# Moving two state updates of a hybrid decoder step from the router's top-4 into the first expert matmuls

## The chip, the cores and the metric

The kernel runs on one core of a Trainium2 chip. The metric is the device time of one execution in microseconds (us). The kernel before took 1251.17 us, the median of three executions (1255.02, 1241.98 and 1251.17 us).

## The reference: what is computed

One inference step of one decoder layer for a prompt group (256 tokens) and a sample group (8 sequences of 4 tokens, 32 tokens), all in float32, with the same weights:

```
x = x + W_out [GatedDeltaNet heads | GLA heads](RMSNorm(x))
x = x + MoE(RMSNorm(x))          # 32 experts, top 4, D = FF = 1024
y = RMSNorm(x)
# GLA, per token:  S_t = diag(e^{gk_t}) S_{t-1} + k_t v_t^T ,  o_t = S_t^T q_t
#   state_gla: (1, 8 sequences, 4 heads, 64, 128), updated and returned as gla_sample
# MoE, per token:  logits = x @ w_router + b_router; top 4; gates = softmax(top 4)
#   gu = x @ w_up[e] + b_up[e]; act = (clip(up)+1) * gate * sigmoid(1.702 gate); act @ w_down[e] + b_down[e]
```

The weights of the 32 experts (w_up 8 MB and w_down 4 MB each) are nearly everything that is read from memory. The new GLA states of the eight sample sequences are an output of their own: nothing later in the layer reads them.

## The kernel before, in words

Each engine has a program written out by hand, and semaphores join them. The first 250 us compute the projections, the convolution and both mixers. Then come the output projection with the router (to about 302 us), and the experts.

**Experts.** They go in 16 pairs (`two_experts`, for both experts of a pair). A pair's weights are twelve units of 2 MB: units 0 to 3 are w_up of the first expert (q = 0), 4 to 7 w_up of the second (q = 1), 8 to 11 w_down. A ring of eight slots holds them (`load_unit`, L362, issued by SyncE). SyncE issues a unit's load when the matmuls that read the slot's last content have signalled (`w_used`, `p_up`, `p_yd`), one after another in one order. In `up` (L1021) a unit, which the change's title calls a piece, is 8 matmuls of 512 columns, recorded as 16; `down` (L1047) is built alike. Between them stand `gather` (L1056: it collects the rows of the tokens that chose the experts, by a matrix `G` of zeros and ones that VectorE writes), transposes (L548) and `scatter` (L972: it adds a pair's result to the tokens).

**The first pair** is written out ahead of the loop. Unit 8 of it doesn't go to the ring: it lies in eight spare places (`extra`, L386), of 256 KB each. Places 6 and 7 are in the buffer `xb`, where the masked keys of the second GLA update (`kgm[1]`) lie until `state_update(5)` has read them; so SyncE waits for `p_up_s` 6 ahead of them.

**State updates.** There are six, 0 to 3 for the delta heads and 4 and 5 for two GLA heads each. `state_update(h)` (L860) does a 32-row outer product per sequence and head into two banks, and signals `p_up_s`. VectorE adds the banks to the decayed state in `states(h)` (L1400: two additions of 128x512) and signals `st_ok`. Updates 4 and 5 use banks 7, 2 and 4, 3. At `st_ok` 6 GpSimd writes `sls` out (L533) and, when that has landed, loads `b_down` in its place (L535), which the last pair needs.

**The router.** VectorE reads the logits (L1487) and makes the top-4 selection in small steps (L1490 to L1502), up to `route_ok`. TensorE waits for this, then counts the positions of the tokens in the experts' lists (L960, L962, signal `p_pos`). VectorE makes `G` of them (L1510 to L1555), TensorE gathers the first half of the rows (L1056, `gather(0, 5)`), ScalarE copies them (L1843), and the first `up` begins. Between its second unit and its third stand `gather(1, 4)`, which writes bank 4 and waits for `st_ok` 6, and `gates_t`. `keep_warm(b, n)` (L556) does n matmuls of the identity with 512 columns into bank b; nobody reads them.

Of the kernel before, what the change touches and what calls it, by code (L numbers as in the profile page):

```python
# [36 lines left out]
def program(nc, a, o):  # L37
    ctx = ExitStack()
    with ctx:
# [3 lines left out]
        def sem(name):  # L43
            return ctx.enter_context(nc.semaphore(name))
# [187 lines left out]
        def used(i, n):  # L232

            name, at = [("w_used", 1), ("w_used", 2), ("w_used", 3), ("p_up", 1), ("w_used", 4), ("w_used", 5), ("w_used", 6), ("p_up", 2),
                        ("w_used", 7), ("p_yd", 1), ("w_used", 8), ("p_yd", 2)][n]
            return name, i * (8 if name == "w_used" else 2) + at

        def place(n, odd, first=False):

            return (n - RING if n > RING else (n + 1) % RING) if first else (n + 4 * odd) % RING  # L240

        def landed(k, n, odd, first=False):

            return (16 if n < RING - 1 else 32) if first else k * 48 + 16 * ((n + 12 * odd) // RING + 1)
# [17 lines left out]
        sems = {n: sem(n) for n in names}  # L262
# [38 lines left out]
        def _(sp):  # L301
# [53 lines left out]
            def load_unit(p, n, odd, first=False):  # L355

                if n < 8:
                    src = up[p * 2 + n // 4, n % 4 // 2, :, UNIT * (n % 2):UNIT * (n % 2 + 1)]
                else:
                    src = dn[p * 2 + (n - 8) // 2, n % 2]  # L360
                s = place(n, odd, first)
                sp.dma_start(slot[WSLOT[s]], src).then_inc(sems[f"ld_w{s}"], 16)  # L362
# [18 lines left out]
            for m in range(8):  # L381
                if m == 2:
                    sp.wait_ge(sems["p_lg"], 3)
                if m == 6:
                    sp.wait_ge(sems["p_up_s"], 6)
                sp.dma_start(extra[m], dn[0, 0, :, 512 * m:512 * (m + 1)]).then_inc(sems["ld_w0" if m == 0 else "ld_extra"], 16)  # L386

            for n in range(9, 12):
                name, value = used(0, n - 9)
                sp.wait_ge(sems[name], value)  # L390
                load_unit(0, n, 0, True)
            for n in range(5):
                name, value = used(0, n + 3)
# [149 lines left out]
        def _(pe):  # L543
# [115 lines left out]
            for t in range(NTT):  # L659
                n = TN[t]  # L660
# [86 lines left out]
            for t in range(NTT):  # L747
                n = TN[t]
# [5 lines left out]
            for k, (l, t) in enumerate(INV):  # L754
                n = TN[t]
# [93 lines left out]
            def state_update(h):  # L849

                pe.wait_ge(sems["kdm_ok"], h + 1)
                for b in range(NB):
                    out_b = bank[ST_BANKS[h][b // 4]]
                    cols = slice((b % 4) * P, (b % 4) * P + P)
                    if h < 4:
                        i = pe.matmul(out_b[:, cols], kdm[h][0:SMP, b, :], vn[0:SMP, 2, h * P:(h + 1) * P], start=True, stop=True)
                    else:
                        for r in range(2):
                            hh = 2 * (h - 4) + r
                            i = pe.matmul(out_b[64 * r:64 * r + 64, cols], kgm[h - 4][b // 4][0:SMP, b % 4, 64 * r:64 * r + 64],  # L860
                                          vg[0:SMP, 2, hh * P:(hh + 1) * P], start=True, stop=True)
                c.tick(i, "p_up_s")
# [28 lines left out]
            def logits(t, j):  # L891

                at = XT.index((t, j))
                if at < 5:
                    pe.wait_ge(sems["xnT_ok"], at + 1)
                else:
                    pe.wait_ge(sems["lgT_ok"], 1)
                for m in range(4 * j, 4 * j + 4):
                    i = pe.matmul(bank[LG_BANKS[t]][0:TN[t], 0:E_N], hT[:, m, TO[t]:TO[t] + TN[t]], wr[:, m, :],
                                  start=m == 0, stop=m == KT - 1, skip_group_check=True)  # L900
                if j == 1:
                    c.tick(i, "p_lg")
# [45 lines left out]
            columns(1, 1)  # L948
            keep_warm(0, 1)
            logits(1, 1)  # L950
            state_update(4)
            state_update(5)

            pe.wait_ge(sems["route_ok"], 1)
            pe.wait_ge(sems["tri_ok"], 3)
# [19 lines left out]
            def gates_t():  # L975

                pe.wait_ge(sems["gat_ok"], 1)
                pe.wait_ge(sems["lg_ok"], 5)
                for t in range(NTT):
                    ins = turn(bank[5][0:E_N, TO[t]:TO[t] + TN[t]], gates[0:TN[t], E_N * t:E_N * (t + 1)], TN[t])  # L980
                ins.then_inc(sems["p_gT"], 1)
# [13 lines left out]
            def up(i, q, k, odd, first=False, last_w=None):  # L995

                pe.wait_ge(sems["sel_ok"], i * 2 + (q + 1))
                for g in range(2):
                    rows_ = slice(64 * g, 64 * g + 64)
                    pe.matmul(bank[2 * q + g][:], sels[q][rows_].rearrange("p h c -> p (h c)"), b_gu[rows_], start=True, stop=False,  # L1000
                              skip_group_check=True)
                for u in range(4):
                    n = 4 * q + u
                    if first and q == 0 and u == 2:
                        pe.wait_ge(sems["st_ok"], 6)
                        gather(1, 4)
                        gates_t()
                    if first and q == 0 and u == 0:
                        pe.wait_ge(sems["lgT_ok"], 2)
                    elif first and q == 0 and u == 1:  # L1010
                        pe.wait_ge(sems["xe_ok"], 1)
                    elif q == 0 and u % 2 == 0:
                        pe.wait_ge(sems["xe_ok"], i * 2 + (u // 2 + 1))
                    s = place(n, odd, first)
                    pe.wait_ge(sems[f"ld_w{s}"], landed(k, n, odd, first))
                    w = slot[WSLOT[s]].rearrange("p (k g h n) -> p k g h n", k=2, g=2, h=2)
                    for kk in range(2):
                        at = 2 * u + kk
                        for g in range(2):
                            for h in range(2):  # L1020
                                last = pe.matmul(bank[2 * q + g][CAP * h:CAP * (h + 1), :], xeT[:, at, q * CAP:(q + 1) * CAP], w[:, kk, g, h, :],  # L1021
                                                 start=False, stop=at == KT - 1, skip_group_check=True)
                    last.then_inc(sems["w_used" if u < 3 else "p_up"], 1)
                    if last_w is not None and u > 0:
                        bias_pair(i, last_w, u - 1)
# [25 lines left out]
            def gather(j, b):  # L1051

                for n in range(4):
                    for t in range(NTT):
                        at = (4 * j + n) * P
                        last = pe.matmul(bank[b][:, n * P:(n + 1) * P], ot[:, t, at:at + P], G[:, t, :], start=t == 0, stop=t == NTT - 1)  # L1056
                last.then_inc(sems["p_gat"], 1)
# [53 lines left out]
        def _(v):  # L1111
# [16 lines left out]
            for t in range(NTT):  # L1128
                n = TN[t]
# [109 lines left out]
            for t in range(NTT):  # L1239
                if t == 1:  # L1240
                    g_diffs(2)
                n = TN[t]
# [11 lines left out]
            for t in range(NTT):  # L1254
                n = TN[t]
                m = upi if t < 2 else upis
                c.done(v.tensor_tensor(Dtt[t], Dtt[t], bc(m.unsqueeze(1), n, H, n), ALU.mult), "d_ok")
            for t in range(NTT):
                n = TN[t]
# [7 lines left out]
            for t in range(NTT):  # L1267
                n = TN[t]
# [14 lines left out]
            for t in range(NTT):  # L1283
                n = TN[t]
# [37 lines left out]
            for k, (l, t) in enumerate(INV):  # L1322
                n = TN[t]
# [71 lines left out]
            def states(h):  # L1395
                v.wait_ge(sems["p_up_s"], h + 1)
                v.wait_ge(sems["dec_ok"], h + 1)
                for k in range(2):
                    st = sgs[:, 4 * k:4 * k + 4, h, :] if h < 4 else sls[:, h - 4, 4 * k:4 * k + 4, :]
                    i = v.tensor_tensor(st, st, bank[ST_BANKS[h][k]][:].rearrange("p (b d) -> p b d", b=4), ALU.add)  # L1400
                c.done(i, "st_ok")
# [82 lines left out]
            for t in range(NTT):  # L1484
                n = TN[t]
# [16 lines left out]
            c.done(v.tensor_tensor(selm[:], gts[:], eqs[:], ALU.add), "route_ok")  # L1502

            c.done(v.memset(posm[:], 0.0), "v_step")
            states(4)
            v.wait_ge(sems["p_pos"], 1)
            for t in range(NTT):
                n = TN[t]
# [3 lines left out]
            def pick_gu(q, e):  # L1512

                v.tensor_copy(sels[q], bc(twos[:, :, bass.ds(e, 1)], P, 2, CAP)).then_inc(sems["sel_ok"], 1)
# [54 lines left out]
            c.done(v.tensor_reduce(cnt[0:1, 0:1], bank[6][0:1, 0:E_N], AX_X, ALU.max), "lg_ok")  # L1569
            for q in range(2):  # L1570
                pick_gu(q, q)
            states(5)
            v.wait_ge(sems["gexp_ok"], 1)
            c.done(v.tensor_tensor(gates[:], gates[:], selm[:], ALU.mult), "v_step")
            c.done(v.tensor_reduce(den[:], e3(gates), AX_X, ALU.add), "v_step")
# [10 lines left out]
            c.done(v.tensor_scalar(cnt[0:1, 1:2], cnt[0:1, 1:2], 1.0, None, ALU.add), "v_step")  # L1586
            c.done(v.tensor_scalar(cgt[0:1, 0:1], cnt[0:1, 1:2], float(PAIRS // 2), -1.0, ALU.mult, ALU.add), "v_step")
            c.done(v.tensor_copy(rnd[:], cgt[0:1, 0:1]), "rnd_ok")

            def two_experts(i, w, first=False, last=False):  # L1590

# [38 lines left out]
            for t in range(NTT):  # L1630
                n = TN[t]
# [276 lines left out]
```

## Time and profile before

| | |
|---|---|
| median of three executions | 1251.17 us |
| profiled execution, its time | 1243.56 us |
| its span (first to last instruction) | 1241.4 us |
| TensorE busy | 97% of the span |
| VectorE, ScalarE, GpSimd busy | 31%, 17%, 6% |
| read from memory | 428.39 MB, written 4.88 MB |

The profile is of one execution. Its page gives the busy time of each engine, the span in 40 slices of 31 us, the chain of work that ended last and the costliest groups of instructions; the trace gives each instruction with its start, its length and what ended the idle time ahead of it. "Landing" is the time from a transfer's issue to its completion. PEclk is TensorE's granted clock as a share of 2.4 GHz.

### The profile page before, as it was taken

To read this page: it belongs to the slowest core of one execution; us is meant where nothing else is said; L and a number is where in the kernel's file an instruction comes from. 1 tells how busy PE (TensorE), PEld (TensorE's weight loads), DVE (VectorE), ACT (ScalarE), POOL (GpSimd) and SP (SyncE) were. 2 spreads that over 40 slices of the span, in tenths; PEclk is the share of its full clock that TensorE was granted. 3 is DMA by queue.
4 is the path that set the end of the run, shared out by engine and by line. 5 is a ranking of instruction groups with operands and counts; after the bars stand their busy time and mean duration, and the time that the engine had idled before them with its cause. 6 is when DMAs were issued, how large, how long until landed. Compare 5 with 4: busy or idle time off the path is not lost.

```text
span 1241.4 us, 15614 instructions
## 1 busy us (share of the span) xinstructions
PE 1207.3 (97%) x6213; PEld 585.8 (47%) x6213; DVE 380.1 (31%) x802; ACT 215.0 (17%) x522; POOL 72.0 (6%) x114
## 2 busy tenths in 40 slices
PE   6999999899999999999999999999999999999997
PEld 5777787766343433434343434334343434243422
DVE  3676774563112130312212121303112121212133
ACT  2143333322120111101020201111010202020102
POOL 5010103251000000000000000000000000000000
PEclk9999999998999999999999999999999999999999
DMA  9423010289999999999999999999999999999993
GB/s 274 129 87 111 31 69 2 73 318 360 404 413 422 428 429 428 429 428 429 428 429 428 428 428 429 429 428 429 428 429 428 428 429 429 428 429 428 428 428 146
DMA packets 50813, 433.75 MB, mean 349 GB/s; under 512 B 7534, under 2 KB 14010, under 8 KB 26332
## 3 DMA queue, kind: packets, MB, share of 16 engines
q1 hardware_dynamic: 49596, 429.46, 83.5%
q0 software_dynamic: 1184, 3.84, 1.0%
q8 instruction: 23, 0.38, 0.1%
q14 instruction: 10, 0.08, 0.0%
HBM read 428.39 MB, written 4.88 MB: 349 GB/s over the span
## 4 chain that ended last, share of the span: by engine, by line
PE 84%; DMA 9%; DVE 4%; ACT 1%; issue 1%; POOL 0%; DVEq 0%; SPq 0%; ACTq 0%; POOLq 0%
PE bank L1021 33%; PE bank L1047 15%; DMA ring<-in_w_up 8%; PE bank L972 7%; PE bank L1056 6%; PE bank L611 4%; PE bank L548 3%; PE bank L703 3%; PE bank L1000 2%; PE bank L872 2%; PE bank L760 1%; PE bank L769 1%; PE bank L767 1%; PE bank L690 1%; PE bank L723 1%
## 5 line engine op out<-in xcount | busy, mean ns | idle before, releaser
L1021 PE MATMUL bank<-ring,xb 128*64 128x512 f32 x2048 | 448.3, 594 | 4.9 <-DMA ring<-in_w_up 4.0
L1021 PEld LDWEIGHTS bank<-ring,xb 128*64 128x64 f32 x2048 | 144.0, 137 | 304.4 <-issue 296.2
L1047 PE MATMUL bank<-ring,qkv 128*64 128x512 f32 x1008 | 223.3, 595 | 0.7 <-ACT qkv L1834 0.7
L1540 DVE TENSOR_TENSOR qkv<-qkv,bank 128x512 f32<-128x512 f32 (+1 forms) x96 | 65.6, 684 | 241.9 <-PE bank L972 241.9
L1047 PEld LDWEIGHTS bank<-ring,qkv 128*64 128x64 f32 x1008 | 69.6, 137 | 130.7 <-issue 126.2
L972 PE MATMUL bank<-xb,wsm 128*128 128x512 f32 (+1 forms) x192 | 92.9, 620 | 1.7 <-DVE xb L1532 0.9
L1056 PE MATMUL bank<-rowsel,ob 128*128 128x128 f32 x768 | 91.9, 276 | 0.0
L1532 DVE COPY xb<-bank 64x512 f32<-64x512 f32 x16 | 11.1, 695 | 260.6 <-PE bank L1047 260.6
L1056 PEld LDWEIGHTS bank<-rowsel,ob 128*128 128x128 f32 x768 | 89.3, 194 | 2.4 <-DVE rowsel L1555 1.6
L1519 DVE TENSOR_SCALAR xb<-bank 128x512 f32<-128x512 f32 x32 | 21.8, 682 | 206.7 <-PE bank L548 188.8
L611 PE MATMUL bank<-hT,ring 128*128 128x288 f32 x320 | 81.0, 413 | 0.0
L1829 ACT ACTIVATE qkv<-xb 128x512 f32<-128x512 f32 x32 | 20.2, 631 | 342.1 <-DVE xb L1519 340.0
L611 PEld LDWEIGHTS bank<-hT,ring 128*128 128x128 f32 x320 | 61.2, 193 | 17.7 <-issue 0.8
L1839 ACT COPY xb<-bank 64x512 f32<-64x512 f32 x48 | 27.8, 579 | 185.7 <-PE bank L1047 185.3
L972 PEld LDWEIGHTS bank<-xb,wsm 128*128 128x128 f32 (+1 forms) x192 | 25.7, 164 | 67.4 <-DVE qkv L1540 41.7
L538 POOL TENSOR_TENSOR rst<-rst,mhalf 128x1 f32<-128x1 f32 x3 | 2.6, 879 | 915.1 <-DVE rst L1622 915.0
L1823 ACT ACTIVATE xb<-bank,wff 128x128 f32<-128x128 f32 x124 | 35.3, 367 | 53.0 <-PE bank L1056 53.0
L1856 ACT COPY wsm<-bank 128x288 f32<-128x288 f32 x16 | 6.4, 398 | 218.4 <-PE bank L548 218.4
L703 PE MATMUL bank<-hT,ring 128*128 128x288 f32 x128 | 41.1, 436 | 0.1
L1000 PE MATMUL bank<-b_gu,hT 64*128 64x512 f32 x128 | 36.1, 641 | 0.0
L548 PE MATMUL bank<-ident,xb 128*128 128x128 f32 x152 | 28.4, 305 | 1.5 <-DVE xb L1130 1.5
L872 PE MATMUL bank<-ring 128*128 128x512 f32 x64 | 28.4, 597 | 0.4 <-DVE ring L1392 0.4
(355 smaller groups left out, 885.3 us busy)
## 6 DMA issues: line engine op xcount, KB each, us to landing
ring<-in_w_up SPq DMA_DIRECT2D x128, 2048.0 KB, 23.0
ring<-in_w_down SPq DMA_DIRECT2D x63, 2048.0 KB, 26.2
ring<-in_w_in SPq DMA_DIRECT2D x7, 2048.0 KB, 8.3
ring<-in_w_out SPq DMA_DIRECT2D x2, 2048.0 KB, 8.3
ring<-in_state_gdn SPq DMA_DIRECT2D x4, 512.0 KB, 10.2
out<-ring POOLq DMA_DIRECT2D x1, 2048.0 KB, 15.1
xb<-in_x_prompt SPq DMA_DIRECT2D x1, 1024.0 KB, 5.2
sls<-in_state_gla SPq DMA_DIRECT2D x4, 256.0 KB, 7.4
```

What stands on the lines that cost most here:

```text
L548: return pe.transpose(out, src, ident[0:n, 0:n])
L611: i = pe.matmul(bank[at % 4][:, 0:T], w[:, k, n * P:(n + 1) * P], hT[:, k, :], start=k == 0, stop=k == KT - 1)
L703: i = pe.matmul(bank[0][:, 0:T], w[:, k, n * P:(n + 1) * P], hT[:, k, :], start=k == 0, stop=k == KT - 1)
L872: i = pe.matmul(bank[b][:], z, w[:, k, :], start=k == 0, stop=k == KT - 1)
L972: pe.matmul(bank[banks[at]][0:TN[t], :], S[:, TO[t]:TO[t] + TN[t]], yr[:, 512 * j:512 * (j + 1)], start=True, stop=True).then_inc(sems["p_ ...
L1000: pe.matmul(bank[2 * q + g][:], sels[q][rows_].rearrange("p h c -> p (h c)"), b_gu[rows_], start=True, stop=False, skip_group_check=True)
L1021: last = pe.matmul(bank[2 * q + g][CAP * h:CAP * (h + 1), :], xeT[:, at, q * CAP:(q + 1) * CAP], w[:, kk, g, h, :], start=False, stop=at = ...
L1047: last = pe.matmul(bank[5 - q][CAP * h:CAP * (h + 1), :], aTs[q][:, kk, CAP * u:CAP * (u + 1)], w[kk][h], start=u == 0 and kk == 0, stop=u ...
L1056: last = pe.matmul(bank[b][:, n * P:(n + 1) * P], ot[:, t, at:at + P], G[:, t, :], start=t == 0, stop=t == NTT - 1)
L1540: v.tensor_tensor(d, d, bank[banks[at]][0:TN[t], :], ALU.add).then_inc(sems["sc_ok"], 1)
L1823: last = act.activation(xeT[:, k, :], bank[b][:, P * n:P * (n + 1)], ACT.Copy, scale=wff[:, k:k + 1])
L1839: act.copy(yr[CAP * q:CAP * (q + 1), 512 * h:512 * (h + 1)], bank[5 - q][CAP * h:CAP * (h + 1), :]).then_inc(sems["yb_ok"], 1)
```

## The change

Three engines are touched. On TensorE `state_update(4)` and `(5)` leave their place ahead of the wait for `route_ok`; four matmuls of `keep_warm` stand there. Both updates now come in the first `up`, between its second and third unit, ahead of the wait for `st_ok` 6 and `gather(1, 4)`. On VectorE `states(4)` and `states(5)` go from among the selection's steps to behind `rnd_ok`, ahead of the first `swiglu`. On SyncE the loads of units 9 and 10 go ahead of `extra` 6 and 7, whose wait for `p_up_s` 6 now ends later.

```diff
@@ SyncE
                 if m == 6:
+                    for n in range(9, 11):
+                        name, value = used(0, n - 9)
+                        sp.wait_ge(sems[name], value)
+                        load_unit(0, n, 0, True)
                     sp.wait_ge(sems["p_up_s"], 6)
                 sp.dma_start(extra[m], ...)
-            for n in range(9, 12):
+            for n in range(11, 12):
                 ...
@@ TensorE
             logits(1, 1)
-            state_update(4)
-            state_update(5)
+            keep_warm(0, 4)
             pe.wait_ge(sems["route_ok"], 1)
 ...
                     if first and q == 0 and u == 2:
+                        state_update(4)
+                        state_update(5)
                         pe.wait_ge(sems["st_ok"], 6)
                         gather(1, 4)
                         gates_t()
@@ VectorE
             c.done(v.memset(posm[:], 0.0), "v_step")
-            states(4)
             v.wait_ge(sems["p_pos"], 1)
 ...
                 pick_gu(q, q)
-            states(5)
             v.wait_ge(sems["gexp_ok"], 1)
 ...
             c.done(v.tensor_copy(rnd[:], cgt[0:1, 0:1]), "rnd_ok")
+            states(4)
+            states(5)
```

TensorE in the first `up`, from the second unit's last matmuls to the third unit. Before (`ring` is a weight slot, `xb` on its left the gathered rows, `rowsel` holds `G`, `ob` the rows of all tokens):

```order
L1021 MATMUL bank1<-ring,xb 64x512 x2
L1056 MATMUL bank4<-rowsel,ob 128x128 [waits st_ok]
L1056 MATMUL bank4<-rowsel,ob 128x128 x11
L548 MATMUL bank5<-ident,ml 32x128 [waits lg_ok,gat_ok]
L1021 MATMUL bank0<-ring,xb 64x512 [waits ld_w3,xe_ok]
```

With the change:

```order
L1026 MATMUL bank1<-ring,xb 64x512 x2
L864 MATMUL bank7<-xb,qkv 64x128 [waits kdm_ok]
L864 MATMUL bank7<-xb,qkv 64x128 x7
L864 MATMUL bank2<-xb,qkv 64x128 x8
L864 MATMUL bank4<-xb 64x128 [waits kdm_ok]
L864 MATMUL bank4<-xb 64x128 x7
L864 MATMUL bank3<-xb 64x128 x8
L1061 MATMUL bank4<-rowsel,ob 128x128 [waits st_ok]
```

The 32 outer products now stand in the middle of a weight stage, and right behind them TensorE waits for VectorE's last addition.

SyncE's loads at the same place. Before:

```order
L386 DMA hT<-in_w_down 128x512 x3
L386 DMA xb<-in_w_down 128x512 [waits p_up_s]
L386 DMA xb<-in_w_down 128x512
L362 DMA ring<-in_w_down 128x4096 [waits w_used] x3
```

With the change:

```order
L390 DMA hT<-in_w_down 128x512 x3
L362 DMA ring<-in_w_down 128x4096 [waits w_used] x2
L390 DMA xb<-in_w_down 128x512 [waits p_up_s]
L390 DMA xb<-in_w_down 128x512
L362 DMA ring<-in_w_down 128x4096 [waits w_used]
```

Two full loads went ahead of the two small ones; the third stays behind.

## Rows read from the trace of the kernel before

**Rows 1.** The page, part 2: TensorE busy and GB/s, in 40 slices of 31 us.
```profile
PE   6999999899999999999999999999999999999997
GB/s 274 129 87 111 31 69 2 73 318 360 404 413 422 428 429 428 429 428 429 428 429 428 428 428 429 429 428 429 428 429 428 428 429 429 428 429 428 428 428 146
```

**Rows 2.** Busy time by stretch: PE, PEld, DVE, ACT, POOL, clock, DMA share, GB/s.
```profile
340.00:362.00 22.00, 22.00 (x129) 11.42 (x127) 3.40 (x8) 5.64 (x14) 0.00 (x0) 1.00 1.01 426
362.00:366.00 4.00, 4.00 (x20) 1.15 (x16) 0.00 (x0) 0.00 (x0) 0.00 (x0) 1.00 0.88 315
```

**Rows 3.** The chain of waits, late in the expert loop: start us, us, what.
```profile
892.59 5.66 PE bank L972 x12
...
949.43 5.66 PE bank L972 x12
...
970.21 33.79 DMA ring<-in_w_up
...
1125.15 5.66 PE bank L972 x12
```

**Rows 4.** The ring load issued at 356.1 us, and its landing.
```profile
L362 SPq DMA_DIRECT2D ring<-in_w_up x1: 356/356/356, 356.1 to 356.1; - x1
...
DMA to landing us min/median/max: 9.0/9.0/9.0
```

**Rows 5.** The next ring load, issued at 362.8 us, and its landing.
```profile
L362 SPq DMA_DIRECT2D ring<-in_w_up x1: 348/348/348, 362.8 to 362.8; - x1
...
DMA to landing us min/median/max: 8.1/8.1/8.1
```

**Rows 6.** The one after it, issued at 366.3 us, and its landing.
```profile
L362 SPq DMA_DIRECT2D ring<-in_w_up x1: 332/332/332, 366.3 to 366.3; - x1
...
DMA to landing us min/median/max: 9.5/9.5/9.5
```

**Rows 7.** TensorE in order of time: start us, us, line, count [idle before it].
```profile
295.97 1.02 PE L556 MATMUL bank<-qkv,ident 128*128 128x512 f32 x2
...
297.93 1.96 PE L860 MATMUL bank<-xb,qkv 32*64 32x128 f32 x32
299.73 1.91 PE L860 MATMUL bank<-xb 32*64 32x128 f32 x32
302.25 0.64 PE L960 MATMUL bank<-ml,tri 128*128 128x32 f32 x2 [0.61 <-DVE ml L1502]
...
304.86 2.08 PE L556 MATMUL bank<-qkv,ident 128*128 128x512 f32 x2
306.96 3.61 PE L1056 MATMUL bank<-rowsel,ob 128*128 128x128 f32 x24
...
311.56 7.09 PE L1021 MATMUL bank<-ring,xb 128*64 128x512 f32 x32
318.58 2.94 PE L1056 MATMUL bank<-rowsel,ob 128*128 128x128 f32 x24
...
322.76 7.09 PE L1021 MATMUL bank<-ring,xb 128*64 128x512 f32 x32 [0.88 <-ACT xb L1823]
```

**Rows 8.** TensorE's granted clock around it: columns as in Rows 2.
```profile
298.15:301.56 3.41, 3.41 (x64) 3.24 (x60) 3.00 (x13) 3.41 (x4) 1.55 (x4) 1.00 0.99 418
301.56:304.97 3.41, 2.80 (x21) 2.40 (x19) 1.99 (x6) 2.51 (x4) 0.00 (x0) 0.50 1.03 437
304.97:308.40 3.43, 3.40 (x9) 1.83 (x9) 3.15 (x14) 0.00 (x0) 0.00 (x0) 0.50 1.01 430
```

**Rows 9.** VectorE in order of time: columns as in Rows 7.
```profile
302.45 1.28 DVE L1400 TENSOR_TENSOR sls<-sls,bank 128x512 f32<-128x512 f32 x2
305.04 0.63 DVE L1510 SCALAR_TENSOR_TENSOR ml<-bank,ml 128x32 f32<-128x32 f32 x3 [1.30 <-PE bank L962]
...
306.22 0.68 DVE L1555 TENSOR_TENSOR rowsel<-slots_io,pp 128x128 f32<-128x128 f32 x3
```

**Rows 10.** SyncE's loads of `extra` 6 and 7, and their landing.
```profile
L386 SPq DMA_DIRECT2D xb<-in_w_down x2: 327/2172/4017, 301.7 to 302.0; - x2
...
DMA to landing us min/median/max: 16.7/17.0/17.3
```

## The prediction

> **What bounds the kernel now.** I read the page first. TensorE is busy at nine tenths or more in nearly every slice, and memory delivers 428 GB/s in nearly every slice from the thirteenth on [rows 1]. Both look full, so the page can't tell which of them sets the end. The chain of waits can. In the loop, as far as about 949 us, a pair takes 949.43 - 892.59 = 56.84 us, and the chain stays on TensorE. The next three pairs take 1125.15 - 949.43 = 175.72 us together, which is 5.20 us more than 3 x 56.84, and there the chain runs through a weight load [rows 3]. At 428 GB/s a unit of 2 MB takes 2.097/0.428 = 4.90 us, and twelve of them 58.8 us, 1.9 more than TensorE's pair. So TensorE is the faster of the two in the loop: it starts behind the loads, catches up, and from the twelfth pair on is fed unit by unit. Behind 1125 us it sets the end again.
>
> What sets the loads' pace, then? They are saturated unless a slot comes free too late. I looked for a hole in them. The load issued at 356.1 us landed at 365.1, the one issued at 362.8 at 370.9, the one issued at 366.3 at 375.8 [rows 4 to 6]. The last two are 4.9 us apart, as the rate wants; the first two are 5.8. In 362 to 366 us the queues moved 315 GB/s where 426 went ahead [rows 2]. So the load at 362.8 came some 0.9 us too late, since TensorE had not freed the slot. Thus the chain of this execution is: TensorE to 362.8 us, the weight loads to about 1121 us, TensorE to the end. Two things follow. **What TensorE loses ahead of 362.8 us shifts all later landings and the end by the same amount**; the 5.20 us that it waits late don't take it up. What it gains there is worth 0.9 us at most, since then the loads have no hole left. The change lies all ahead of 362.8 us, so I need its sum for TensorE there: call it S.
>
> **The place that is left.** The two updates are 1.80 + 1.91 = 3.7 us of TensorE, from 297.93 to 301.64 us, and behind them it idles 0.61 us for VectorE's selection [rows 7]. The route's end, 302.2 us, doesn't depend on them. Taking them away gives nothing by itself. The four spare matmuls take at most 4 x 1.02 = 4.1 us [rows 7], and end by 302.0, within the selection: cost 0 under that cover, 4.1 us without it.
>
> VectorE's two additions between `route_ok` and `p_pos` (1.28 us from 302.45) ended ahead of its 1.30 us wait for TensorE [rows 9]; taking them away gives 0. The second pair of additions came behind `G`, on no path that `up` waits for: 0.
>
> What can be gained is the clock. It was at 1.2 GHz from 301.56 to 308.40 us, right behind the updates [rows 8]. In it the position matmuls ran from 302.25 to 304.86, 2.6 us, and the first gather took 3.61 us where the second one, at 2.4 GHz, took 2.94 [rows 7]. The spare matmul between them took 2.08 instead of 1.02, but it lies beside VectorE's 1.9 us from `p_pos` to `G` (305.04 to 306.90, [rows 9]). If the clock stays up, the position matmuls save between 0 and half of 2.6, I take 0.7, and the gather 0.7. If it falls at the position matmuls anyway (they are small, and an idle stretch stands ahead of them), nothing is saved. Bounds 0 and 2.0 us (1.3 + 0.7), I take **-1.0 us**.
>
> The Trainium skill's page "TensorE: Matmul & The Clock Gate" (Terms) prices throttled time at the time x (1 - K/N), here 6.8 us x 1/2 = 3.4 us; by it S would be 2.4 us smaller than mine. The rows above show that part of the dip covered idle time and VectorE's steps.
>
> **The place that is new.** Between the second and third unit TensorE does the same 32 products, 3.7 us, and nothing is beside them: **+3.7 us**. Then it waits for `st_ok` 6. Before, that was long there when `gather(1, 4)` came. Now the additions of update 4 (1.28 us) hide behind the products of update 5, and those of update 5 don't: a pair of additions took 1.28 us [rows 9], and a step across engines cost about 0.1 us (`route_ok` and `p_pos` both), twice: **+1.45 us**, bounds 1.3 and 1.6. Behind it stand `gather(1, 4)`, `gates_t`, and every later unit; ScalarE's copy, for which the third unit waited 0.88 us [rows 7], comes as late as the gather does, so that wait stays.
>
> The clock again: the updates ran with TensorE busy in 3.41 of 3.41 us, and the clock fell at the end of that stretch [rows 8]. Now 3.7 us of them and 1.4 us of idling follow each other, so I expect one fall there. If it comes, the gather costs 0.7 more, and if it lasts into the third unit that goes at half pace. Bounds: no fall, 0; a fall as long as before, at half pace for all of 6.8 us, 3.4. I take **+1.25 us**, the gather's 0.7 and half a microsecond of the third unit. The skill's page "TensorE: Matmul & The Clock Gate" (What's actually happening) says that activity releases the throttle, a busy engine staying at full clock; by that rule alone this term is 0 and S is 1.25 us smaller. The first stretch of rows 8 speaks against it: all busy, and down.
>
> **Queues passed.** SyncE now holds `extra` 6 and 7 until `p_up_s` 6, about 321 us instead of 301.7, behind units 9 and 10. They landed 17 us after issue [rows 10], so at about 338 us; the first `down`, the only reader, stands behind six more units, 21 us from the third unit's start (322.76 before, [rows 7]), so at 344 us or later before and later still now. Cost 0. Units 9 and 10 wait for the same signals as before. Unit 11 and all behind it wait for TensorE, whose lateness is S already. The four writes of `sls` and the load of `b_down` go some 13 us later, into the loads of 323 to 327 us; ahead of 362.8 us that only fills room, and the reader of `b_down` is the last pair: 0. VectorE's additions come before its first `swiglu`, for which TensorE needs two more units: 0.
>
> **Sum.** S = -1.0 + 3.7 + 1.45 + 1.25 = **+5.4 us**, from 3.0 (-2.0 + 3.7 + 1.3) to 8.7 (3.7 + 1.6 + 3.4). Against the profiled execution that is 1243.56 + 5.4 = 1249.0 us; against the median of the three others 1256.6. The four executions shown spread over 13 us, far more than S, and their mean is 1247.9; a new median may fall anywhere among them, so I set the forecast at 1247.9 + 5.4 = **1253 us**.
>
> **Rivals.**
> - *The lateness is hidden (0.16).* If the loads have no hole at 362.8 us, for instance since memory is a little slower in a run of 1251 us than in this one, TensorE's lateness is first taken up by the depth of the queue, and its 5.20 us of late waits take the rest. For it: the hole is only 0.9 us, and the chain's longest part is the loads [rows 2, 3]. Against it: with S = 5.4 the slots come so late that a hole opens even there; only 1 to 2 us would be hidden. In full it gives S = 0, about 1248 us.
> - *The early gain wins (0.04).* The clock stays up at both places, TensorE arrives earlier by 2 us, and the updates cost less in the middle of wide matmuls than alone. It would need the 3.7 us to shrink below 0.5; S is then -0.9 at best, 1247 us. The rows speak for 3.7.
> - *The clock stays down (0.05), the other side.* Place: from the third unit on. If, behind 5 us of narrow products and waiting, the clock doesn't return with the gather but stays at 1.2 GHz through the third to sixth unit, these 14.2 us (2 x 7.09, [rows 7]) double: S = 4.15 + 0.7 + 14.2 = 19, 1267 us. It decides from some 8 us of such work on, where S passes 12.5. For it: the dip of rows 8 outlasted the updates by 6.8 us. Against it: it ended as soon as a gather ran.
> - *The late `extra` (0.03).* A load late in the run takes 33.8 us to land [rows 3]; if these two did so here, they would come at 355 us, up to 5 us after `down` wants them (344 + 5.4 at the earliest): up to 1258 us.
>
> The forecast's own case has 0.72.
>
> **Range and chances.** 1243 to 1262 us: the lowest execution shown with most of the least S hidden, up to the highest, 1255, with S at 7. A change under 1% (12.5 us) can't be told from none for this kernel. The forecast and the two rivals with a small S lie within it; beyond it on the slow side is the clock rival with 0.05, and as much for the spread of the medians on top of 5.4 us; beyond it on the fast side only that spread, 0.02.
>
> **What would show it.** In the new profile: spare matmuls at 298 to 301.5 us and no idle time changed ahead of L963; PEclk at 1.00 in 302 to 308 if the first gain is real, and the first `up` starting at about 310.5 instead of 311.56. The updates at about 317.6 to 321.3, then a wait of about 1.4 us on VectorE's `sls`, and a stretch at clock 0.5 between 319 and 326. The third unit at about 328 instead of 322.76. The ring load that was issued at 362.8 at about 368, with its landing 8 us behind it; and the scatter that began at 1125.15 at about 1130.5. I am wrong if the third unit is late but that scatter isn't (hidden), or if the clock is still down at 330 us.

## The result, and the profile after

| | before | with the change |
|---|---|---|
| median of 20 executions each | 1248.08 us | 1252.95 us |
| lowest and highest | 1241.98, 1257.62 | 1249.20, 1263.80 |
| profiled execution, its time | 1243.56 us | 1251.58 us |
| its span | 1241.4 us | 1249.5 us |

The ratio of the changed kernel to the kernel before is 1.0058, with a 95% interval from 1.0036 to 1.0079: 7.2 us slower, from 4.5 to 9.9. The medians lie 4.9 us apart. The forecast was 1253 us: slower, by less than 1%.

The two traces show where it goes. TensorE with the change, in order of time, answers to [rows 7]:

```profile
299.57 3.68 PE L560 MATMUL bank<-qkv,ident 128*128 128x512 f32 x8
303.99 0.41 PE L963 MATMUL bank<-ml,tri 128*128 128x32 f32 x2 [0.73 <-DVE ml L1507]
...
305.60 1.12 PE L560 MATMUL bank<-qkv,ident 128*128 128x512 f32 x2
307.70 5.49 PE L1061 MATMUL bank<-rowsel,ob 128*128 128x128 f32 x24 [0.98 <-DVE rowsel L1559]
313.12 1.32 PE L1003 MATMUL bank<-b_gu,hT 64*128 64x512 f32 x4
314.37 7.09 PE L1026 MATMUL bank<-ring,xb 128*64 128x512 f32 x32
321.39 1.96 PE L864 MATMUL bank<-xb,qkv 32*64 32x128 f32 x32
323.18 1.91 PE L864 MATMUL bank<-xb 32*64 32x128 f32 x32
326.54 4.57 PE L1061 MATMUL bank<-rowsel,ob 128*128 128x128 f32 x24 [1.45 <-DVE sls L1405]
330.95 0.51 PE L552 MATMUL bank<-ident,ml 128*32 128x128 f32 x3
332.34 7.09 PE L1026 MATMUL bank<-ring,xb 128*64 128x512 f32 x32 [0.88 <-ACT xb L1828]
```

The third unit of the first `up` starts at 332.34 us, 9.58 later than before. Piece by piece:
- 1.74 us were lost ahead of the change (303.99 against 302.25). They are no part of it: the section on the hardware comes back to them.
- From the first position matmul to the first unit of `up` it took 10.38 us (314.37 - 303.99), before 9.31 (311.56 - 302.25): +1.07. The position matmuls went faster (1.6 us instead of 2.6), then TensorE idled 0.98 us, and the gather took 5.49 us instead of 3.61.
- From the end of the second unit to the second gather stand 5.15 us that weren't there (321.39 to 326.54): 3.7 of products and 1.45 of waiting for `sls`.
- That gather took 4.57 us instead of 2.94, and to the third unit it was 5.80 instead of 4.18: +1.62.

I call the stretch from the first position matmul to the third unit **the route**. It was 302.25 to 322.76 = 20.51 us, and is 28.35: **+7.84 us by the change**.

The granted clock with the change (columns as in [rows 2]):

```profile
303.99:306.90 2.91, 2.73 (x20) 1.70 (x20) 1.12 (x7) 1.73 (x3) 0.00 (x0) 0.97 1.00 422
306.90:313.70 6.80, 6.00 (x26) 5.68 (x28) 4.00 (x25) 0.47 (x2) 0.00 (x0) 0.51 0.97 380
313.80:327.30 13.50, 12.05 (x106) 6.44 (x103) 2.57 (x4) 0.57 (x3) 0.52 (x1) 1.00 0.75 286
327.50:330.80 3.30, 3.30 (x18) 3.30 (x18) 0.00 (x0) 0.00 (x0) 2.02 (x3) 0.53 0.94 367
```

The first fall didn't go away: it began at about 306.7 us, 2.7 us behind the first position matmul, where in [rows 8] it began 0.7 us ahead of it. It is as long as there, 6.8 us, but now the whole first gather lies in it. A second fall of 3.4 us, from 327.2 us, hit the second gather.

The loads, against [rows 5] and [rows 3]. The ring load that was issued at 362.8 us, and the late end of the chain of waits:

```profile
L362 SPq DMA_DIRECT2D ring<-in_w_up x1: 348/348/348, 372.4 to 372.4; - x1
...
DMA to landing us min/median/max: 7.4/7.4/7.4
```

```profile
959.01 5.66 PE bank L975 x12
979.79 33.82 DMA ring<-in_w_up
...
1134.76 5.66 PE bank L975 x12
```

The load is 9.6 us late, and the scatter that began at 1125.15 us is 9.61 us late. TensorE's late waits took up nothing. The span is longer by only 8.1: late in the kernel before the clock fell for a short while and the last scatter but one took 7.25 us, and here there was no such fall and it took 5.72.

### The profile page after: what moved, and what is told of

It is laid out like the page before. It is cut to its first block, busy times and chain, and to the rows that moved or that the text cites. A ratio compares the mean times of both kernels' runs of the same rounds, so it can differ in the third digit from the quotient of the medians.

```text
span 1249.5 us, 15629 instructions
## 1 busy us (share of the span) xinstructions
PE 1213.6 (97%) x6221; PEld 590.5 (47%) x6221; DVE 380.0 (30%) x802; ACT 214.9 (17%) x522; POOL 72.2 (6%) x114
## 4 chain that ended last, share of the span: by engine, by line
PE 84%; DMA 9%; DVE 5%; ACT 1%; issue 1%; POOL 0%; DVEq 0%; SPq 0%; ACTq 0%; POOLq 0%
PE bank L1026 33%; PE bank L1052 15%; DMA ring<-in_w_up 8%; PE bank L975 7%; PE bank L1061 6%; PE bank L615 4%; PE bank L552 3%; PE bank L707 3%; PE bank L1003 2%; PE bank L876 2%; PE bank L764 1%; PE bank L773 1%; PE bank L771 1%; PE bank L694 1%; PE bank L727 1%
## 5 line engine op out<-in xcount | busy, mean ns | idle before, releaser
L1061 PE MATMUL bank<-rowsel,ob 128*128 128x128 f32 x768 | 95.4, 283 | 2.4 <-DVE sls L1405 1.4
L1061 PEld LDWEIGHTS bank<-rowsel,ob 128*128 128x128 f32 x768 | 92.7, 200 | 3.5 <-DVE rowsel L1559 1.8
```

## The experiments

Each but e4 and e8 is judged by the route in its own profiled execution, since the executions of one kernel spread over 7 to 19 us, and the route leaves out what happened ahead of it. The route repeats well: e8 leaves that part of the kernel before as it was and has 20.50 us, e4 has 20.85, where the kernel before has 20.51. Each kernel has one trace. The excerpts are TensorE in order of time unless said otherwise.

How far a longer route arrives is read from the scatter that began at 1125.15 us before, 822.90 us behind the route's start. In nine of the ten traces with other work on the route (the changed kernel and all runs but e4 and e8) its shift agrees with the route's within 0.5 us; e7 is the tenth.

**e1: the updates left out** (the output `gla_sample` isn't computed).

```diff
# the changed kernel
-                    sp.wait_ge(sems["p_up_s"], 6)
+                    sp.wait_ge(sems["kdm_ok"], 6)
...
-            g.wait_ge(sems["st_ok"], 6)
...
-                        state_update(4)
-                        state_update(5)
-                        pe.wait_ge(sems["st_ok"], 6)
...
-            states(4)
-            states(5)
```

The waits of SyncE and GpSimd for the updates had to go with them.

> The changed kernel with GLA sample updates 4 and 5 left out on TensorE and VectorE (that state output is then not computed); the four spare matmuls stay. Measure: from the first position matmul to the third unit of the first up, called the route. It was 20.51 us before (302.25 to 322.76) and 28.35 with the change (303.99 to 332.34). Theory A (3.7 us of products and 1.45 us of waiting are paid, and the clock falls once early and once behind the updates): the route is 28.35 - 5.15 - 1.63 = 21.6 us if the early fall stays, 19.5 or less if it doesn't come, and the time is within 1 us of the kernel before. Rival B (the lateness of the change comes from elsewhere, the loads' order or the transfers of the states): the route stays above 25 us.

```profile
311.55 0.41 PE L962 MATMUL bank<-ml,tri 128*128 128x32 f32 x2 [0.73 <-DVE ml L1503]
...
315.26 5.49 PE L1057 MATMUL bank<-rowsel,ob 128*128 128x128 f32 x24 [0.98 <-DVE rowsel L1555]
...
328.93 2.94 PE L1057 MATMUL bank<-rowsel,ob 128*128 128x128 f32 x24
...
333.10 7.09 PE L1022 MATMUL bank<-ring,xb 128*64 128x512 f32 x32 [0.88 <-ACT xb L1822]
```

Route 21.55 us: 6.80 us of the 7.84 belong to the updates' new place. The other 1.04 stay with the spare matmuls in: the first gather still takes 5.49. So the early fall needs no update. Rival B is out. The time's ratio is 0.9968 (0.9942 to 0.9995), 0.6 to 7.2 us below the kernel before, though the route is 1.04 longer and the late scatter comes 1.05 us later behind the route's start. The route doesn't account for that, and its cause stays open.

**e2: the updates one unit earlier.**

```diff
# the changed kernel
+                    if first and q == 0 and u == 1:
+                        state_update(4)
+                        state_update(5)
                     if first and q == 0 and u == 2:
-                        state_update(4)
-                        state_update(5)
                         pe.wait_ge(sems["st_ok"], 6)
```

> The changed kernel with both updates one place earlier, between the first and second unit, so that VectorE's additions lie beside the second unit. Theory A: the wait of 1.45 us for the additions is gone, 3.7 us of products stay, and without the idle time the clock may hold: route 25.3 to 26.9 us, against 28.35 with the change; a ring load that is issued late at the end of the first pair, and the end, come earlier by the same 1.5 to 3 us. Rival B (the wait is only moved, to ScalarE's copy or the second unit's load): route 28 us or more.

```profile
302.60 0.41 PE L963 MATMUL bank<-ml,tri 128*128 128x32 f32 x2 [0.74 <-DVE ml L1508]
...
316.57 1.96 PE L864 MATMUL bank<-xb,qkv 32*64 32x128 f32 x32
318.37 1.91 PE L864 MATMUL bank<-xb 32*64 32x128 f32 x32
320.21 3.65 PE L1027 MATMUL bank<-ring,xb 128*64 128x512 f32 x16
323.79 2.94 PE L1062 MATMUL bank<-rowsel,ob 128*128 128x128 f32 x24
...
327.97 7.09 PE L1027 MATMUL bank<-ring,xb 128*64 128x512 f32 x32 [0.88 <-ACT xb L1829]
```

Route 25.37 us, 2.98 less than with the change. Both the wait and the second fall are gone; the gather takes 2.94. The late scatter begins at 1130.83 us, 828.23 behind the route's start, 2.54 us less than with the change. Ratio 1.0013 (0.9979 to 1.0046).

**e7: the wait taken away, the place kept.**

```diff
# the changed kernel
-        ST_BANKS = [..., (7, 2), (4, 3)]
+        ST_BANKS = [..., (7, 2), (6, 3)]
                         state_update(5)
-                        pe.wait_ge(sems["st_ok"], 6)
                         gather(1, 4)
...
+                if first and q == 1:
+                    pe.wait_ge(sems["st_ok"], 6)
                 pe.wait_ge(sems["sel_ok"], i * 2 + (q + 1))
```

> The changed kernel with update 5 in banks 6 and 3 instead of 4 and 3, so that the second gather needn't wait for VectorE's additions; the wait stands ahead of the second expert's up. Place of the updates unchanged. Theory A: the wait of 1.45 us is gone, and without idle time behind the products there is no second clock fall (1.6 us), as with the updates one unit earlier: route 25.3 us against 28.35. Rival (the fall comes from the products alone): route 26.9 us.

```profile
305.04 0.41 PE L963 MATMUL bank<-ml,tri 128*128 128x32 f32 x2 [0.74 <-DVE ml L1508]
...
324.19 1.91 PE L864 MATMUL bank<-xb 32*64 32x128 f32 x32
326.03 2.94 PE L1062 MATMUL bank<-rowsel,ob 128*128 128x128 f32 x24
...
330.21 7.09 PE L1027 MATMUL bank<-ring,xb 128*64 128x512 f32 x32 [0.89 <-ACT xb L1829]
```

Route 25.17 us. The products alone, at the same place, bring no second fall; products with the wait behind them did, in the changed kernel and in e5. Ratio 1.0006 (0.9976 to 1.0036), at most 4.5 us, while the trace has more. In this execution the loads lost another 1.4 us behind the route (its counterpart of the scatter at 1125.15 us is 6.1 us late against the route's 4.7). The trace shows where: the ring load issued at 373.7 us landed 12.7 us later, 6.5 us behind the one before it. Why is open.

**e5: the idle time ahead of the first gather filled.**

```diff
# the changed kernel
-            keep_warm(5, 1)
+            keep_warm(5, 2)
```

> The changed kernel with two spare matmuls instead of one between the position matmuls and the first gather, in the 0.98 us that TensorE idled there. Route as before (first position matmul to third unit of the first up). Theory A (the early clock fall comes since TensorE's small matmuls and this idle time follow each other): the clock holds, the first gather takes 2.9 us instead of 5.5, route about 25.8 instead of 28.35. Rival C (the 32-column position matmuls alone bring the fall): the gather stays at 5.5 us and the route at 28.3.

```profile
312.63 0.41 PE L963 MATMUL bank<-ml,tri 128*128 128x32 f32 x2 [0.74 <-DVE ml L1507]
...
314.24 1.98 PE L560 MATMUL bank<-qkv,ident 128*128 128x512 f32 x4
316.34 2.94 PE L1061 MATMUL bank<-rowsel,ob 128*128 128x128 f32 x24
...
332.45 4.57 PE L1061 MATMUL bank<-rowsel,ob 128*128 128x128 f32 x24 [1.44 <-DVE sls L1405]
...
338.25 7.09 PE L1026 MATMUL bank<-ring,xb 128*64 128x512 f32 x32 [0.88 <-ACT xb L1828]
```

Route 25.62 us, 2.73 less. With one more spare matmul in the 0.98 us of idle time the clock stayed up through the first gather; the second fall stayed. Rival C is out. Its median, 1255.7 us, and its ratio, 1.0033 (0.9996 to 1.0071), don't show the gain: it is smaller than their spread.

**e9: both mends together** (e5's and e7's edits).

> The changed kernel with both mends together: two spare matmuls ahead of the first gather, and update 5 in banks 6 and 3 with no wait ahead of the second gather. Theory A (the losses add up: 2.7 us of early fall, 1.45 of waiting and 1.6 of second fall go, 3.7 us of products stay): route 25.17 - 2.73 = 22.4 us, still 1.9 above the 20.51 of the kernel before. Rival (the falls hang together, so that a clock held early falls at the products): 24 us or more.

```profile
307.87 2.94 PE L1062 MATMUL bank<-rowsel,ob 128*128 128x128 f32 x24
...
322.46 2.94 PE L1062 MATMUL bank<-rowsel,ob 128*128 128x128 f32 x24
```

Route 304.15 to 326.63 = 22.48 us, as the sum of the parts said. Both gathers take 2.94 us, and the granted clock is 1.00 throughout. Ratio 1.0008 (0.9970 to 1.0046).

**e11: the floor** (e1 with e5's edit; the output `gla_sample` isn't computed).

> Updates 4 and 5 left out (that state output isn't computed), four spare matmuls beside the top-4 and two ahead of the first gather: the floor of this stretch. Theory A: no fall, route 21.55 - 2.73 = 18.8 us, 1.7 us below the kernel before; so that much is what the updates cost there by the clock. Rival: 20.5 us, the updates of before cost nothing.

```profile
305.69 2.94 PE L1057 MATMUL bank<-rowsel,ob 128*128 128x128 f32 x24
```

Route 301.97 to 320.81 = 18.84 us. So the kernel before pays 1.67 us for its clock fall, and e9, with no fall and no wait, is 3.64 above the floor: the products, 3.7 us, at their price. Ratio 0.9985 (0.9950 to 1.0020). The counterpart of the scatter at 1125.15 us comes 821.62 us after the route's start, against 822.90 before: of 1.67 us gained, 1.28 arrive there. The prediction's ceiling for a gain was 0.9 us; the 0.4 us above it are within the half microsecond of agreement.

**e3: wide work in the same place**, on the kernel before.

```diff
# the kernel before, first up, ahead of the wait for st_ok
+                        keep_warm(7, 6)
                         pe.wait_ge(sems["st_ok"], 6)
                         gather(1, 4)
```

> The kernel before, with six matmuls of the identity (512 columns) ahead of the second gather of the first up: 6 x 0.88 = 5.3 us of wide work on TensorE, no update moved. Theory A (TensorE's time ahead of the late ring load shifts the end one for one): route 20.5 + 5.3 = 25.8 us, the scatter that began at 1125.15 begins 5.3 us later, the time is 5.3 us (0.4%) longer. Rival H (the 5.2 us of late waits for loads take it up): the route grows, the scatter and the time don't.

```profile
303.65 0.63 PE L960 MATMUL bank<-ml,tri 128*128 128x32 f32 x2 [0.61 <-DVE ml L1503]
...
319.95 5.42 PE L556 MATMUL bank<-qkv,ident 128*128 128x512 f32 x12
325.21 2.84 PE L1057 MATMUL bank<-rowsel,ob 128*128 128x128 f32 x24
...
329.28 7.09 PE L1022 MATMUL bank<-ring,xb 128*64 128x512 f32 x32 [0.88 <-ACT xb L1824]
```

Route 25.63 us, +5.12. From the route's start to the counterpart of the scatter at 1125.15 it is 828.48 us instead of 822.90, +5.58: all of it arrives, and half a microsecond more. Rival H would have 0. The clock stays up behind this wide work (the gather takes 2.84 us), so the loss is the work's length alone. Ratio 1.0029 (0.9999 to 1.0059), which is 3.6 us and holds 5.3.

**e8: wide work behind the late load**, on the kernel before.

```diff
             two_experts(0, 0, 0, 0, first=True)
+            for _ in range(4):
+                pe.matmul(bank[0][:], ident[:], b_gu[:], start=True, stop=True)
```

> The kernel before, with four matmuls of the identity (512 columns) at the end of the first pair, right behind the late ring load. Four such cost 4.2 us on TensorE (1.06 each, as measured in the loop). Theory A (behind the late load the loads have 1.4 us of slack, which is least at the load issued at 391.6 us, and it takes up that much of the lateness): from the first position matmul to the scatter of 1125.15 us 822.9 + 2.8 = 825.7 us. Rival H (all of it is hidden by the 5.2 us of late waits): 822.9. Rival T (one for one as ahead of the hole): 827.1.

The chain of waits of e8 (start us, us, what); its route began at 309.84 us and took 20.50:

```profile
960.65 5.66 PE bank L972 x12
...
1038.36 34.31 DMA ring<-in_w_up
...
1135.13 5.65 PE bank L972 x12
```

The first of these scatters is 650.81 us behind the route's start, before it was 949.43 - 302.25 = 647.18: TensorE was 3.63 us late there. The last is 825.29 behind it, against 822.90: 2.39 us late. So 1.24 of the 3.63 us were taken up, near the 1.4 that the slack of one load allowed (with 3.63 in place of 4.2 it would have been 2.2 late). Neither rival fits, and the difference is more than twice the half microsecond of agreement, but it rests on one trace. Ratio 1.0018 (0.9980 to 1.0056).

**e4: wide work in every pair of the loop**, on the kernel before.

```diff
# up(), every pair but the first
+                if not first and q == 1:
+                    pe.matmul(bank[2 * q][:], ident[:], b_gu[:], start=True, stop=True)
```

> The kernel before, with one matmul of the identity (512 columns) in every pair but the first, ahead of the second expert's up: 15 x 0.88 = 13 us of TensorE, all behind the late ring load. Theory A (from there to the last pairs the loads set the pace, and TensorE's 5.2 us of waits and 1.9 us a pair take it up): the time grows by 1 to 2 us only, and the waits of L1021 for loads begin later or shrink. Rival T (TensorE sets the end throughout): 13 us longer, 1.05%.

```profile
1077.11 5.66 PE bank L972 x12
1135.01 5.66 PE bank L972 x12
```

This expectation (1 to 2 us) missed, by a fault of its arithmetic: it let TensorE take up the 5.2 us of waits and 1.9 us a pair besides, and the two are largely the same room. The chain of e4 has no load in it any more; a pair takes 57.90 us (1135.01 - 1077.11), 1.06 more than before, and TensorE sets the pace to the end. Thirteen pairs at 1.06 are 13.8 us; less the 5.20 us of waits that the kernel before had there, 8.6 remain. Measured from the route's start (303.20) to 1135.01: 831.81 us against 822.90, of which 0.34 is its longer route: +8.57. That fits 5.20 us as all the room there is in the loop up to there. Rival T, by which all of the 13.8 us would arrive, is out too. Ratio 1.0043 (1.0012 to 1.0074).

**e6 and e10: the updates in the two gaps that cost nothing**, on the kernel before.

```diff
# e6                                  # e10
-            state_update(4)
-            state_update(5)
+            state_update(4)          # keep_warm(0, 1); state_update(4);
+            keep_warm(0, 2)          # keep_warm(0, 1)
...
-            keep_warm(5, 1)
+            state_update(5)
```

> The kernel before, with update 4 and two spare matmuls beside the top-4, and update 5 beside VectorE's steps to G, in place of the spare matmul there; no work in the first up. Theory A: both gaps still cover their 3.7 and 1.9 us, so nothing is added; the clock falls later or not at all: route 19.0 to 20.5 us against 20.51 before. Rival C (narrow products in both gaps bring the fall just ahead of the gather): the gather takes 5.5 us, route 21.5 to 22.

> As the kernel with update 4 beside the top-4 and update 5 beside the steps to G, but with one spare matmul on either side of update 4. Theory A (narrow products, position matmuls and update 5 stand in a row of over 5 us in any order, so a fall comes at the first gather): route 20.4 us as there. Rival (the wide matmul right ahead of the position matmuls breaks the row): 19.0 us, the first that beats the 20.51 of before.

e6:

```profile
309.38 1.96 PE L860 MATMUL bank<-xb 32*64 32x128 f32 x32
311.48 4.54 PE L1056 MATMUL bank<-rowsel,ob 128*128 128x128 f32 x24
```

e10:

```profile
309.67 0.41 PE L961 MATMUL bank<-ml,tri 128*128 128x32 f32 x2 [0.36 <-DVE ml L1503]
...
311.28 2.84 PE L860 MATMUL bank<-xb 32*64 32x128 f32 x32
314.05 5.30 PE L1057 MATMUL bank<-rowsel,ob 128*128 128x128 f32 x24
...
331.54 7.09 PE L1022 MATMUL bank<-ring,xb 128*64 128x512 f32 x32 [0.88 <-ACT xb L1824]
```

e6: route 307.76 to 328.20 = 20.44 us, the first gather 4.54. e10: 21.87 us, the gather 5.30, and update 5 itself went slower at the low clock (2.84 us instead of 1.91). In both the gaps cover the products, and a fall of the clock just ahead of the gather takes the gain back. e6's route is within what its theory expected, at the upper end, but the fall is the one that its rival C named, 3.4 us long and so not at the rival's full price (5.5 us for the gather). For e10 the theory was wrong by 1.5 us, and its rival by more. Ratios 0.9974 (0.9935 to 1.0014) and 0.9995 (0.9962 to 1.0029): no version here that keeps all outputs is shown to beat the kernel before.

## Why the prediction was right, point by point

- **What bounds the kernel: right.** TensorE's lateness ahead of the late ring load shifts the end one for one. With the change the load and the later scatter moved by 9.6 us alike, e3 showed it with work that changes neither the clock nor the order of the transfers, and e8 showed that the same kind of work behind that load is partly taken up. The rival "the lateness is hidden", at 0.16, is out.
- **The new place, +3.7 and +1.45: right to 0.01 us.** 321.39 to 326.54 are 5.15 us. e9 against e11 gives 3.64 for the products alone.
- **The clock behind the updates, +1.25: right in kind, 1.62 measured.** One fall came, 3.4 us long, and all it cost was the gather's; the third unit took 7.09 us as before, where the prediction gave it half a microsecond. By the rule on the price of throttled time in the Trainium skill's page "TensorE: Matmul & The Clock Gate" (Terms) 3.4 us x 1/2 is 1.7 us, and the trace agrees. The rule on a busy engine (What's actually happening), by which this term would be 0, is not borne out as plainly as I read it: in e7 TensorE was busy throughout and the clock held; in the kernel before it was busy just as long and the clock fell. No trace says what made the difference.
- **The place that is left, -1.0: wrong, +1.07 measured.** This is the step that failed. It said: "If the clock stays up, the position matmuls save between 0 and half of 2.6, I take 0.7, and the gather 0.7", with bounds 0 and -2.0. The position matmuls did save 1.0 us. But the same speed shortened the single spare matmul behind them, which the prediction took as lying beside VectorE's steps and so as worth nothing. The sign that was named, the clock at 1.00 from 302 to 308 us and the first `up` at about 310.5, failed: the clock was down from about 306.7, and `up` began at 314.37. With 0.98 us of idle time behind the spare matmul the clock fell 3.4 us later than before, counted from the first position matmul, on the gather instead of on small matmuls and waiting. The gather's price was too small as well: the 0.7 us come from a gather of 3.61 us of which only the first 1.4 lay below full clock (306.96 to 308.40); wholly in a fall it took 5.49, which is 2.55 more than 2.94. e5 shows what the idle time was worth: one more spare matmul there is worth 2.73 us, and then the term would have been -1.66 (1.07 - 2.73), inside the bounds.
- **The sum: 7.84 instead of 5.4**, within 3.0 to 8.7. Against the profiled execution before, 1.74 us more were lost ahead of the change and 1.53 fewer at the end, neither by the change.
- **The queues, 0: right for the end, with a hole that was not foreseen.** No reader of `extra` 6 and 7 waited. But with 0.5 MB less in the queue and units 9 and 10 later, the loads ran dry for a while, as this stretch of the changed kernel shows:

```profile
315.20:318.60 3.40, 3.40 (x18) 1.15 (x16) 0.00 (x0) 0.00 (x0) 0.00 (x0) 1.00 0.06 20
```

  20 GB/s. It cost nothing, since the load at 372.4 us waits for TensorE in any case: TensorE waited for no weight load between 300 and 400 us.
- **The time: 1253 forecast, 1252.95 measured.** That nearness is luck in part: two terms of the sum were off by 2.07 and 0.37 us, and the rest is how the executions fell. I had put the median before at 1247.9 from four executions (20 gave 1248.08), and 5.4 us on top lies between the 4.9 of the medians and the 7.2 of the ratio.

## What to carry to other kernels

When an engine and the loads are both nearly full, look for the last load that is issued late because a slot wasn't free: here TensorE's time ahead of it went into the end in full, its time behind it only beyond the slack. A step that stands beside a wait on another engine costs little there (here 1.67 us, by the clock), and its full length once it is moved into a stream of work, plus any wait that comes with it. Spare matmuls have to be counted at the clock they are meant to hold: what fills a gap at 1.2 GHz leaves half of it open at 2.4.

## What the runs showed of the hardware

- The granted clock fell behind a stretch of small matmuls with 0.98 us of idle time in it (changed kernel, e1, e2, e7: first gather 5.49 us) and not when the idle time was filled (e5, e9, e11: 2.94 us). Idle time isn't needed for a fall: in the kernel before, it came while TensorE was busy in 3.41 of 3.41 us [rows 8], and in e6, where the same gap was filled with the narrow products of update 5 instead of a matmul of 512 columns, at 311.4 us, and the gather took 4.54. What decides it is open. A fall of 6.8 us cost 2.73 us on a path of gathers, and 1.67 us in the kernel before, where it covered waiting too. The Trainium skill's page "TensorE: Matmul & The Clock Gate" (Terms) would price both at 3.4.
- Much of the spread between executions arises ahead of the experts. Over the 13 traces the first position matmul began between 301.97 and 312.63 us, and the spans lie between 1238.3 and 1256.8. In the traces compared here the clock made the difference. The first position matmul began at 302.25 us in the profiled execution before, 303.99 in that of the change and 311.55 in that of e1, which are alike up to the top-4. In e1 a stretch that holds the same matmuls went at 0.70 of the clock, against 0.91 before:

```profile
200.00:240.00 40.00, 37.52 (x162) 28.30 (x161) 9.14 (x16) 10.58 (x18) 4.69 (x3) 0.70 0.08 25
```

  The 1.74 us of the changed kernel's execution are of this kind: its eight matmuls of the small projection, at 19.80 us, took 5.80 us instead of 4.11, at 0.71 of the clock instead of 1.00.
